# The core of a retention layer: reading out, squaring and scaling four heads in another order

## The reference

```python
proj = hn @ w_in                      # q, k: 4 heads x 256; v, gate: 4 heads x 512
q, k = apply_rope(q), apply_rope(k) * DK ** -0.5
o = (q k^T * decay) v                 # per head; decay is 0 for keys of later chunks
mu = jnp.mean(o, axis=-1)
var = jnp.mean(jnp.square(o - mu), axis=-1)
on = (o - mu) * lax.rsqrt(var + GN_EPS) * gn_g
h = h + (jax.nn.silu(gate) * on) @ w_o
```

## Time and profile before

| | |
|---|---|
| median of 3 runs | 1558.58 us (1558.41 to 1560.11) |
| the profiled execution's own time | 1556.98 us |
| its span, first to last instruction | 1555.1 us |
| mean granted TensorE clock | 0.945 of full speed |
| busy share of PE, DVE, ACT, POOL | 89%, 46%, 34%, 14% |

### The profile page before, as it was taken

One profiled execution on the slowest core, in us unless ns is written; L12 is line 12 of the kernel. 1 busy time (PEld: TensorE's weight loads), 2 busy tenths in 40 slices (PEclk: granted clock), 3 DMA queues, 4 the chain that ended last, 5 costly groups with the idle time before them and its releaser, 6 DMA issues.

```text
span 1555.1 us, 27615 instructions
## 1 busy us (share of the span) xinstructions
PE 1388.3 (89%) x11858; PEld 1167.3 (75%) x11858; DVE 720.4 (46%) x1208; ACT 527.0 (34%) x813; POOL 210.8 (14%) x173
## 2 busy tenths in 40 slices
PE   7999899897677677677999989999999999999997
PEld 7998568664344344344887979999999876899997
DVE  5365665421111121122764665555556564565644
ACT  6346453110000010012334444444345433544442
POOL 5132002100000000001000023211224200101123
PEclk9999899699888889887999999999999999999999
DMA  9332118989999999999435241454355321445340
GB/s 360 138 149 70 68 55 354 378 373 427 430 428 429 428 429 428 429 428 379 187 147 192 109 176 55 163 196 166 112 214 188 139 109 55 163 166 212 121 180 28
DMA packets 32422, 360.01 MB, mean 231 GB/s; under 512 B 5328, under 2 KB 8400, under 8 KB 10192
## 3 DMA queue, kind: packets, MB, share of 16 engines
q1 hardware_dynamic: 32336, 358.76, 57.6%
HBM read 357.70 MB, written 1.05 MB: 231 GB/s over the span
## 4 chain that ended last, share of the span: by engine, by line
PE 70%; DMA 18%; DVE 4%; ACT 3%; issue 2%; SPq 1%; POOL 1%; DVEq 0%; ACTq 0%
PE PS L541 42%; DMA expert_w<-in_w 18%; PE PS L554 5%; PE PS L995 4%; PE PS L589 3%; PE PS L1016 3%; PE PS L960 1%; DVE wl L1936 1%; SPq L395 1%; PE PS L1175 1%; PE PS L837 1%; PE PS L572 1%; PE PS L1369 1%; ACT wh L1428 1%; PE PS L694 1%
## 5 line engine op out<-in xcount | busy, mean ns | idle before, releaser
L1936 DVE TENSOR_TENSOR wl<-raw,wh 128x4096 fp32r<-128x4096 f32 (+2 forms) x67 | 272.0, 4059 | 207.4 <-ACT wh L1428 207.4
L1428 ACT ACTIVATE wh<-raw 128x4096 fp32r<-128x4096 f32 (+2 forms) x67 | 223.1, 3330 | 117.3 <-PE PS L541 111.8
L541 PE MATMUL PS<-UH,wh 128*128 128x272 f32 (+1 forms) x840 | 244.5, 291 | 14.0 <-DVE wl L1992 10.6
L541 PE MATMUL PS<-UH,wl 128*128 128x272 f32 (+1 forms) x840 | 241.5, 288 | 0.0
L541 PE MATMUL PS<-UL,wh 128*128 128x272 f32 (+1 forms) x840 | 241.0, 287 | 0.0
L995 PE MATMUL PS<-expert_w,XW 128*32 128x256 f32 x2048 | 159.1, 467 | 89.3 <-DMA expert_w<-in_w 89.0
L995 PEld LDWEIGHTS PS<-expert_w,XW 128*32 128x32 f32 x2048 | 71.1, 129 | 165.2 <-DMA expert_w<-in_w 109.3
L541 PEld LDWEIGHTS PS<-UH,wh 128*128 128x128 f32 x840 | 159.1, 189 | 15.3 <-DVE wl L1992 10.6
L541 PEld LDWEIGHTS PS<-UL,wh 128*128 128x128 f32 x840 | 159.5, 190 | 0.4
L541 PEld LDWEIGHTS PS<-UH,wl 128*128 128x128 f32 x840 | 159.2, 190 | 0.0
L2300 DVE TENSOR_TENSOR SG<-PS,SG 128x128 f32<-128x128 f32 x32 | 9.3, 292 | 274.0 <-ACT SG L1695 274.0
(11 more groups left out here) (522 smaller groups left out, 3011.1 us busy)
## 6 DMA issues: line engine op xcount, KB each, us to landing
expert_w<-in_w SPq DMA_DIRECT2D x96, 2048.0 KB, 20.4
raw<-in_up SPq DMA_DIRECT2D x22, 2048.0 KB, 8.4
raw<-in_down SPq DMA_DIRECT2D x16, 1408.0 KB, 6.0
raw<-in_ret_v SPq DMA_DIRECT2D x4, 2048.0 KB, 8.7
raw<-in_ret_gate SPq DMA_DIRECT2D x4, 2048.0 KB, 8.4
raw<-in_ret_o SPq DMA_DIRECT2D x4, 2048.0 KB, 9.4
raw<-in_ret_qk SPq DMA_DIRECT2D x3, 2048.0 KB, 8.6
raw<-in_w_in_ga SPq DMA_DIRECT2D x2, 2048.0 KB, 8.4
```

Source lines behind the costliest of these rows:

```text
L541: mm = pe.matmul(gbank(g)[:, c0:T], w[:, c:c + P], x(k)[:, c0:], start=(k == 0 and j == 0), stop=(k == nk - 1 and j == 2))
L1428: act.activation(WH[n % 2][:, 0:w], raw(n)[:, 0:w], ACT.Copy).then_inc(hi_done, 1)
L1936: dve.tensor_tensor(wl_of(n)[:, 0:w], raw(n)[:, 0:w], WH[n % 2][:, 0:w].bitcast(F32), ALU.subtract).then_inc(lo_done, 1)
```

## The change

- PE: `ret_squares(0)` stands ahead of `ret_values(1)`, `ret_squares(1)` ahead of `ret_values(2)`, `ret_squares(2)` in the middle of `ret_values(3)`, and `ret_squares(3)` behind the first two of the sixteen steps of `ret_out` instead of behind eight.
- ACT: the root of head h stands ahead of `ret_read(h + 1)`. In `ret_read(h)`, from the third head on, the wait for all four `RLO` of head h - 2 is replaced by a wait for block v's `RLO` ahead of block v.
- ACT: before the slab split ahead of `ret_read(0)`, a root of one column into the unused tile `RCOL`. The slab is split in four quarters.
- DVE: the four gate units' loop is moved behind the definition of `weigh`, and `weigh(0)` stands ahead of taking the last gate unit (j = 15) out of its bank. The slab's low part is made in quarters, three of them after `weigh(1)` and the last after `weigh(3)`.

```diff
-            def ret_values(h):
+            def ret_values(h, units=range(4)):
...
-                for v in range(4):
+                for v in units:
...
             ret_scores(2)
+            ret_squares(0)
             ret_values(1)
-            ret_squares(0)
             ret_scores(3)
+            ret_squares(1)
             ret_values(2)
-            ret_squares(1)
-            ret_values(3)
+            ret_values(3, range(0, 2))
             ret_squares(2)
-            ret_out(0, 8)
+            ret_values(3, range(2, 4))
+            ret_out(0, 2)
             ret_squares(3)
-            ret_out(8, 12)
-            ret_out(12, 16)
+            ret_out(2, 16)
...
-                hi(n + 2 * RH + s + 2)
+                if s == 3:
+                    c = GAINS["eps_heads"]
+                    root_mean(RCOL[:, 0:1], gains[:, c:c + 1], RV, "eps_heads")
+                    for q in range(4):
+                        hi_part(n + 2 * RH + 5, q)
+                else:
+                    hi(n + 2 * RH + s + 2)
...
                 if h >= 2:
-                    act.wait_ge(rlo_done, 4 * (h - 1))
                     act.wait_ge(gr_done, h - 1)
                 for v in range(4):
                     g = UNIT0["ro"] + 4 * h + v
+                    if h >= 2:
+                        act.wait_ge(rlo_done, 4 * (h - 2) + v + 1)
...
             for h in range(RH):
+                act.wait_ge(gv_mm, h + 1)
+                root_mean(GRS[:], sbank(3)[:, 0:T], RV, "eps_heads").then_inc(gstd, 1)
                 if h + 1 < RH:
                     ret_read(h + 1)
-                act.wait_ge(gv_mm, h + 1)
-                root_mean(GRS[:], sbank(3)[:, 0:T], RV, "eps_heads").then_inc(gstd, 1)
...
+                    dve.wait_ge(unit_done, g + 1)
+                    if j == 15:
+                        weigh(0)
+                    freeing(dve.tensor_tensor(GATE[:, j, :], gbank(g)[:, 0:T], rs[:], ALU.mult))
...
-            dve.wait_ge(unit_done, UNIT0["gate"] + 16)
-            weigh(0)
...
-            lo(n + 2 * RH + 5)
+            for q in range(3):
+                lo_part(n + 2 * RH + 5, q)
             for h in range(RH):
                 if h + 2 < RH:
                     weigh(h + 2)
+                if h == 1:
+                    lo_part(n + 2 * RH + 5, 3)
```

More of the change, by code:

```diff
@@ L2398, in silu @@
                                          in1=GSIG[j % 2][:], op0=ALU.mult, op1=ALU.mult).then_inc(gate_t, 1)
[L2400 to L2409, removed]
             def weigh(h):
@@ L2422, in weigh @@
                         .then_inc(st_done, 1)
-            dve.wait_ge(unit_done, UNIT0["gate"] + 16)
-            weigh(0)
+            for s in range(4):
+                for u in range(4):
+                    j = 4 * s + u
+                    g = UNIT0["gate"] + j
+                    dve.wait_ge(unit_done, g + 1)
+                    if j == 15:
+                        weigh(0)
+                    freeing(dve.tensor_tensor(GATE[:, j, :], gbank(g)[:, 0:T], rs[:], ALU.mult))
+                    if j:
+                        silu(j - 1)
+                if s < 3:
+                    lo(n + 2 * RH + s + 2)
             silu(15)
```

## The result

| | before | changed |
|---|---|---|
| median | 1558.68 us (4 runs) | 1546.28 us (1543.93 to 1547.14, 4 runs) |
| the profiled execution's own time | 1556.98 us | 1543.93 us |
| its span | 1555.1 us | 1542.1 us |
| stretch, last gate product to second output slab | 52.01 us | 42.98 us |

The ratio of the changed kernel's time to that of the kernel before is 0.9916, with an interval of 0.9899 to 0.9933. The forecast was 1549.6 us (0.9942 of the median it started from) with a range from 1548.2 to 1552.6, so the kernel became faster as forecast, but by more than the range allows. The two traces differ by 13.0 us of span. The stretch gives 9.0 of them, and the prediction said 8.95; the rest lies ahead of the stretch (it starts 3.95 us earlier), in code that is the same in both kernels.

What follows compares the result with a forecast made beforehand. PE was taken to bound the kernel, busy 89% of the span. 0.77 + 8.68 - 0.5 = 8.95 us off 1556.98 gave 1548.0, plus 1.6 to the median: 1549.6 us, range 1548.2 to 1552.6.

Steps and rivals of the forecast that it cites:

- The floor: PE's own work in the stretch once its waits and slow clock are taken off 52.01 us: 41.8 us.
- the five losses: PE's lost time in the stretch: 1.54, 0.86, 4.60, 1.63 (reduced clock) and 1.59 us, 10.22 us in all.
- Weighing head 0 first: On DVE at the stretch's start: PE starts the scores of head 1 earlier, gain 0.77 us.
- ACT before the first read-out: Table load, one-column root and four quarters delay head 0's read-outs: new PE wait 0.5 us, ends 0.2 and 1.3.
- about 1380 ns of draining: Rival: draining behind ACT's table load makes PE wait 1.4 us longer before squares 0; 1551.0 us, 4%.
- Squares early, root early, lap broken: Later heads on PE and ACT: losses of 0.86, 4.60, 1.63 and 1.59 us go, gain 8.68 us.
- The place named as the tightest: Output steps 0 and 1 need banks of head 3's first two read-outs, free about 927.7, needed 927.9: spare 0.2 us.
- POOL slowed: Rival: POOL's low parts become the brake, up to 7.3 us a head, squares 3 late; 1551.6 us, 12%.
- The lap did not stay: Rival: the lap through ACT, DVE and POOL stays at 9.85 us, gain only 3.8 us; 1554.8 us, 5%.
- nothing was given back behind it: Rival: the gain is lost behind the stretch, by a slab not split in time; 1558.6 us, 4%.
- the clock's rival: PE's clock falls to 1.2 GHz at its first stops and stays there; 1583.6 us, slower, 3%.
- the last of the sum: Step from the profiled execution's forecast 1548.0 us to the median's 1549.6, adding the same 1.6 us difference as before.

Runs made afterwards that it cites:

- late table load: The changed kernel without the one-column root ahead of the slab split, which is whole again as before: mean 1548.31 us (16 runs).

## Why the prediction was right and wrong

**The floor and the five losses.** Right. Work of 41.8 us and two waits, 0.78 and 0.42 us, give 43.0; the forecast for the length was 43.1 and four traces have 42.98 to 43.00.

**Weighing head 0 first.** Right as a row, wrong as a worth. PE started 0.78 us behind the last gate product instead of 1.54, as said. But my sum booked 0.77 of gain here and 0.5 of loss on ACT as two things, and the experiment shows that the second hangs on the first: without the early weighing there is no wait before the squares, so of the 0.77 only 0.30 are left.

**ACT before the first read-out.** The one-column root took 0.30 us, starting its successor after 0.20; four quarters took 3.88 in all. The new wait on PE is 0.42 us. The kernel with the late table load has no wait there, and its PE comes from the scores at 905.05 to the squares at 907.07, which is 2.02 us; here 901.76 + 2.02 = 903.78, and the squares start at 904.20. The forecast was 0.5, but the prediction's own terms give it better than it said: 900.70 + 1.28 + 0.2 + 3.8 + 2.23 - 0.2 = 908.0 and not 908.1, against 907.6, so 0.4. Its ends of 0.2 and 1.3 do not follow from its rows either; those give 0.0 and 1.1. Between the table load's end and the next operation lie 0.01 us. The Trainium skill ("ScalarE: Activation LUTs", "What ACT_TABLE_LOAD costs") has about 1380 ns of draining there; neither kernel's row shows it (914.71 to 914.73 in the earlier trace rows, 898.05 to 898.06 here). What I missed is that this part, as a whole, costs time in the stretch: ACT waits nearly 2 us for PE ahead of the first root, and the load fitted there.

**Squares early, root early, lap broken.** Right. Roots of heads 1 to 3 came 19.32, 27.21 and 32.66 us behind the start of the stretch; the forecast of 918.0, 926.0 and 931.4 was 19.1, 27.1 and 32.5 behind 898.86. The place named as the tightest, output steps 0 and 1, held: the values ended and the output began 923.97 - 920.03 = 3.94 us behind the start of the squares of head 2, and the squares (1.89) and half of the values (2.02) fill 3.91 of them.

**The rivals.** POOL slowed to 4.95 us for one head and nobody waited. The lap did not stay, the clock in the stretch stayed full, and nothing was given back behind it. Against the clock's rival the prediction held that only the wait of 4.45 us had been followed by the low level. With PE's order alone a wait of 1.75 us was too, so the four traces of the changed kernel show the full clock for waits of 0.62 and 0.26 us, and say nothing of longer ones.

**The step that failed** is the last of the sum, from the profiled execution to the median, and with it the width of the range. Two terms were mis-sized.

First, the clock's loss in the kernel before, 1.63 us in the sum. That is what the one trace had; three of four have 2.6. So the stretch is worth 9.7 us on average, and 10.0 against those three, where the sum has 8.95. "I take the same difference from it" hid this. If most executions are like those three, 1 us of the 1.6 us between the profiled execution and the median lay in the stretch itself and went with the change.

Second, the scatter. I put "some 0.7 us" of scatter of the median below the forecast, from three runs within 1.7 us of each other. Single runs of the kernel before spread from 1551.1 to 1563.1, with 2.3 us as their standard deviation, so a median of three or four moves by more than 1 us from this alone. The median that the sum started from, 1558.58, stood 1.0 us above the mean of 111 runs.

With the stretch's 9.7 us off the mean of 1557.6, the changed kernel stands at 1547.9, already below my range of 1548.2. Of the 3.3 us between 1549.6 and the measured 1546.28, some 0.8 are the stretch, 1.0 the median started from, 0.2 the four runs against the mean of 22, and the last 1.4, to the mean of 1546.45, are open. The range should have reached down to 1545 or so.

## What to carry to other kernels

Where several engines pass a tile around in a ring, compute the lap from one row and compare it with the bottleneck's own work per item: here 9.85 us against 7.89. Change the order on both ends together, since one end alone gave next to nothing (a ratio of 0.9985) and the other half. Taking parts back one by one shows what each is worth while the others stand, and here that was 2.9 us of 9.2: where two parts break the same lap, take both back in one run too. A helper that starts earlier is worth only what the bottleneck waits for it, so look first at whether the engine already idles where it stands: in the stretch the early table load did not need its early place. And take the spread of a kernel's single runs from more than three of them before a range is drawn.

## What was not expected of the hardware

- Filling a wait of 4.6 us on PE with useless products made the stretch of the kernel before 2.4 us shorter (50.51 against 52.90 to 53.01 in three of four traces). The wait cost 1.6 or 2.6 us more than its length, depending on whether the low level lasted 3.4 or 6.8 us.
- The length of a wait alone does not tell whether the low level follows. With PE's order alone it followed waits of 1.75 and 2.85 us, for 3.4 us each; without PE's order it did not follow one of 1.88. What decides between them is not shown.
- The part behind the stretch takes 604.2 to 604.4 us or 607.3 to 607.5 us in 14 of 18 traces (the others 605.6, 605.8, 605.9 and 606.0), and the clock at one later place of latent attention tells the two groups apart.
